# A two-layer decoder trunk with expert retrieval: choosing the experts of a token tile by groups of heads, and the second tile's one step later

## What is computed

```python
h = _rms(x, g_mix); z = h @ w_in            # q/k/v, latents, conv channels, gates
y_d = differential attention; y_m = latent attention; y_c = short gated convolution
x = x + (sum_i sigmoid(gate_i) * (branch_i @ W_branch_i)) @ w_out
x = x + _peer(_rms(x, g_ffn), w_query, sub_keys, u_experts, v_experts)
x = x + jax.nn.sigmoid(_rms(x, g_ple) @ w_ple_gate) * (p_i @ w_ple_proj)
```

```python
q = (hc @ w_query).reshape(T, PEER_HEADS, 2, PEER_DK)               # 8 heads, 2 halves
s = jnp.einsum('thpd,phnd->thpn', q, sub_keys)                      # 128 keys a half
top_s, top_i = lax.top_k(s, K_SUB)                                  # 16 of 128
cand = (top_s[:, :, 0, :, None] + top_s[:, :, 1, None, :])          # 16 x 16 sums
best_s, best_c = lax.top_k(cand.reshape(..., 256), PEER_TOPK)       # 16 of them
expert = i1 * N_KEYS + i2; gate = jax.nn.softmax(best_s, axis=-1)
act = jax.nn.gelu(jnp.einsum('thkd,td->thk', u_tab[expert], hc))
out = jnp.einsum('thk,thkd->td', gate * act, v_tab[expert])
```

## Time and profile before

| | |
|---|---|
| Median of 3 runs (lowest, highest) | 3680.86 us (3680.29, 3682.27) |
| Profiled execution: its time, its span | 3685.88 us, 3684.1 us |
| Busy: TensorE, VectorE, ScalarE, POOL | 2899.2, 2490.3, 1434.9, 1336.4 us |
| Moved by DMA | 1298.54 MB, mean 352 GB/s over the span |
| of it gathered rows | 1073.81 MB |
| Granted clock of TensorE, mean | 0.898 |

### The profile page before, as it was taken

How to read it: one execution, slowest core, us unless ns; L and a number is a source line. 1 busy time by engine, 2 the same in 40 slices (tenths; PEclk the granted TensorE clock), 3 DMA queues, 4 the chain that set the end, 5 groups by cost and what they waited for, 6 DMA issues and landing times. The chain is left out here.

```text
span 3684.1 us, 28841 instructions
## 1 busy us (share of the span) xinstructions
PE 2899.2 (79%) x8144; PEld 1478.3 (40%) x8144; DVE 2490.3 (68%) x5165; ACT 1434.9 (39%) x3967; POOL 1336.4 (36%) x1033
## 2 busy tenths in 40 slices
PE   7689948878988788867988788878998785656556
PEld 4454714535436333533436334535436331112112
DVE  1311386877667877777667877877667976777775
ACT  2230224457433344457433344457433342224222
POOL 0000033434333443345332443344332444555553
PEclk9879979989999999889999999989999897778777
DMA  4213379999998999999998999999998999999996
GB/s 155 83 69 139 113 310 376 390 363 387 401 381 343 387 398 403 387 390 405 420 376 346 391 408 398 370 384 421 417 389 342 399 399 421 422 421 397 422 421 254
DMA packets 182400, 1298.54 MB, mean 352 GB/s; under 512 B 20320, under 2 KB 21856, under 8 KB 26592
## 3 DMA queue, kind: packets, MB, share of 16 engines
q0 software_dynamic: 147456, 1073.81, 71.9%
q1 hardware_dynamic: 34784, 222.88, 15.3%
HBM read 1294.51 MB, written 2.10 MB: 352 GB/s over the span
## 5 line engine op out<-in xcount | busy, mean ns | idle before, releaser
L548 POOL DMA_INDIRECT ring<-in_uv,experts x1024 | 1333.9, 1303 | 2299.6 <-DVE x L1261 906.2
L1378 PE MATMUL ps_sum<-ring,diag 128*128 128x512 f32 x2120 | 1216.0, 716 | 622.7 <-ACT diag L815 621.9
L1252 DVE SCALAR_TENSOR_TENSOR ring<-ring,h_ffn 128x1024 f32<-128x1024 f32 x1024 | 1233.8, 1220 | 207.5 <-DMA ring<-in_uv,experts 201.3
L1378 PEld LDWEIGHTS ps_sum<-ring,diag 128*128 128x128 f32 x2120 | 437.7, 221 | 1288.2 <-ACT diag L815 892.9
L1261 DVE SCALAR_TENSOR_TENSOR x<-ring,weight,x 128x1024 f32<-128x1024 f32 x494 | 633.2, 1282 | 234.4 <-ACT weight L809 234.3
L807 ACT ACTIVATE dots<-dots 128x1 f32<-128x1 f32 x1024 | 205.3, 200 | 1346.7 <-DVE ring L1252 1344.4
L1516 PE MATMUL ps_act<-area_h,wt 128*128 128x256 f32 x1536 | 347.5, 385 | 2.4 <-ACT area_h L564 2.4
L1644 PE MATMUL ps_act<-wt,area_h 128*128 128x512 f32 x768 | 339.2, 596 | 9.2 <-DMA wt<-in_weights 9.1
L1516 PEld LDWEIGHTS ps_act<-area_h,wt 128*128 128x128 f32 x1536 | 295.0, 193 | 59.2 <-issue 15.6
L809 ACT ACTIVATE weight<-dots,gate 128x1 f32<-128x1 f32 x1024 | 301.6, 295 | 33.3
L1440 PE MATMUL ps_act<-wt,area_h 128*128 128x512 f32 (+1 forms) x704 | 303.7, 591 | 4.8 <-ACT area_h L564 4.5
(11 more groups left out here) (187 smaller groups left out, 2086.8 us busy)
## 6 DMA issues: line engine op xcount, KB each, us to landing
wt<-in_weights SPq DMA_DIRECT2D x190, 1024.0 KB
ring<-in_uv,experts POOLq DMA_INDIRECT x1024
wt<-in_weights SPq DMA_DIRECT2D x11, 512.0 KB
wt<-in_weights SPq DMA_DIRECT2D x4, 768.0 KB
x<-in_x SPq DMA_DIRECT2D x4, 512.0 KB, 5.0
area_y<-in_keys SPq DMA_DIRECT2D x4, 512.0 KB, 9.7
area_f<-in_keys SPq DMA_DIRECT2D x4, 512.0 KB, 10.7
area_f<-in_ffn_rows SPq DMA_DIRECT2D x4, 512.0 KB, 3.2
```

What stands on the lines that cost most here:

```text
L548: pool.indirect_dma_start(ring[:, row.slot, :], None, a[f"uv{row.step // 2}"][:, :], bass.IndirectOffsetOnAxis(ap=experts[:, row.step % 2, ...
L1252: dve.scalar_tensor_tensor(u, u, 1.0, h_ffn[:, row.tile, :], ALU.mult, ALU.mult, accum_out=dots[:, row.j:row.j + 1]).then_inc(dots_ready, 1)
L1378: ins = pe.matmul(ps_sum[:, b, :], diag[:, row.pe_before % DIAGS, :], ring[:, row.slot, D + b * 512:D + (b + 1) * 512], start=row.pe_first ...
```

## The change

The choice is cut otherwise. A part is now (`kind`, first head, end head): `first` makes the sums, maxima and indices of a group of heads, `second` the removal and second eight of it, and four `final` parts follow for all heads. Tile 0 of every chunk is chosen in the groups 0 to 3, 4 and 5, 6 and 7 (`early`), and the first four parts stand behind the ranks of heads 3, 4, 5 and 6. Tile 1 of chunks 1 and 2 is chosen in the step after, in eight parts that stand between `ple_out` and the second `conv_c`, without rows of their own (`topk_late`); that of chunk 3 at the beginning of step 3, with rows; that of chunk 0 where it was. Some temporaries of the choice move from `area_h` to `area_b` and `area_y`. `PE_PART` of `query`, `scores` and `rank` goes from 0.5 to 0.9, and the row costs of `query` and `rank` go up a little.

```diff
-TOPK_OPS = [3, 16, 16, 16, 4, 4, 4]
+LISTS = {"all": (0, 4, 8), "early": (0, 4, 6, 8)}
+FINAL_OPS = [9, 4, 4, 4]
+def parts_of(way):
+    ends = LISTS[way]
+    out = [(kind, lo, hi) for lo, hi in zip(ends, ends[1:]) for kind in ("first", "second")]
+    return out + [("final", i, 0) for i in range(len(FINAL_OPS))]
...
-    "out": 3.5, "ffn_norm": 4, "query": 1.6, "scores": 0.5, "rank": 1.6, "topk": 3,
+    "out": 3.5, "ffn_norm": 4, "query": 2, "scores": 0.5, "rank": 1.8, "topk": 3, "topk_late": 0,
...
-           "out": 0, "query": 0.5, "scores": 0.5, "rank": 0.5, "topk": 1, "taps": 1, "diff_sq": 1, "diff_norm": 1,
+           "out": 0, "query": 0.9, "scores": 0.9, "rank": 0.9, "topk": 1, "taps": 1, "diff_sq": 1, "diff_norm": 1,
...
+def behind(stages, places):
+    out = []
+    for st in stages:
+        out.append(st)
+        for place, more in places:
+            out += more if st == place else []
+    return out
...
+    if stage[0] == "topk":
+        kind, lo, hi = stage[3]
+        return 2 if kind == "final" else 0.6 * (hi - lo)
...
-        out += [("rows", done, i) for i in range(2)] + tail(done + 1, 0)
+        out += choice(step, 1) + [("rows", done, i) for i in range(2)] + tail(done + 1, 0)
...
-        out += choice(d, 0)
-        if d:
-            out += choice(d, 1)
+        first = choice(d, 0, way="early")
+        out = behind(out, [(("rank", d, i), [part]) for i, part in zip((3, 4, 5, 6), first)]) + first[4:]
+    if 0 < step < STEPS - 1:
+        late = choice(step, 1, "topk_late")
+        turn = [st for st in out if st[0] == "diff_turn"][-1]
+        places = [("ple_out", done, 0), ("x_norm", d), ("qkv", d, 0), ("qkv", d, 0), ("qkv", d, 2), turn, ("conv_c", d, 0), ("conv_c", d, 1)]
+        out = behind(out, [(place, [part]) for place, part in zip(places, late)])
...
-        top_f = area_h[:, 512:768].rearrange("p (h c k) -> p h c k", h=HEADS, c=2)
+        top_f = area_b[:, 4096:4352].rearrange("p (h c k) -> p h c k", h=HEADS, c=2)
...
-                        sp.wait_ge(dve_ops, WHERE[("topk", STEPS - 1, 1, len(TOPK_OPS) - 1)].dve + 4)
+                        sp.wait_ge(dve_ops, WHERE[("topk", STEPS - 1, 1, LAST_PART)].dve + 4)
```

More of the change, by code:

```diff
@@ L133, in tiles_done, with choice @@
     return [("for_act", at.evacs + 2)]
-def choice(d, t):
-    return [("topk", d, t, part) for part in range(len(TOPK_OPS))]
+def choice(d, t, name="topk", way="all"):
+    return [(name, d, t, part) for part in parts_of(way)]
+def behind(stages, places):
[5 more added lines that the diff above has]
+    return out
 def mix(d, pairs):
@@ L798, in _ @@
                          branch_more=nothing, mix_turn=mix_turn,
-                         out=out, rows=nothing, tail_norm=tail_norm, tail_out=tail_out, ffn_norm=ffn_norm, query=query, scores=scores, rank=nothing, topk=topk)
+                         out=out, rows=nothing, tail_norm=tail_norm, tail_out=tail_out, ffn_norm=ffn_norm, query=query, scores=scores, rank=nothing, topk=topk, topk_late=topk)
             rows = Rows()
@@ L1230, in _ @@
                          branch_first=branch, branch_more=branch,
-                         mix_turn=nothing, out=out, rows=nothing, tail_norm=tail_norm, tail_out=tail_out, ffn_norm=ffn_norm, query=nothing, scores=nothing, rank=rank, topk=topk)
+                         mix_turn=nothing, out=out, rows=nothing, tail_norm=tail_norm, tail_out=tail_out, ffn_norm=ffn_norm, query=nothing, scores=nothing, rank=rank, topk=topk, topk_late=topk)
             rows = Rows()
@@ L1713, in _ @@
                          branch_more=branch, mix_turn=mix_turn,
-                         out=out, rows=nothing, tail_norm=tail_norm, tail_out=tail_out, ffn_norm=ffn_norm, query=query, scores=scores, rank=nothing, topk=nothing)
+                         out=out, rows=nothing, tail_norm=tail_norm, tail_out=tail_out, ffn_norm=ffn_norm, query=query, scores=scores, rank=nothing, topk=nothing, topk_late=nothing)
             pe.wait_ge(consts_loaded, 16 * N_CONSTS)
```

78 lines of the change are left out of this document (42 added, 36 removed).

## The result

The changed kernel takes 3700.65 us (median of five, 3695.68 to 3707.47) against 3681.34 for the kernel before: ratio 1.0051, 95% interval 1.004 to 1.0062. It is slower by half a per cent. The profiled execution has a time of 3707.47 us and a span of 3705.5 against 3684.1; it is the slowest of the five, 6.8 us above their median, so a few us of what its windows show belong to this execution alone. Both kernels move 1298.5 MB.

What follows compares the result with a forecast made beforehand. The kernel was taken as a stream near its limit with holes where another engine paces it. Prologue -6, step 0 (18 + 2 - 30), steps 1 and 2 (22 + 2 - 30) each, step 3 +4: -24, so 3657 us; range 3608 to 3706.

Steps and rivals of the forecast that it cites:

- C: Queries, ranks and choices of steps 0 to 2, up to the next step's first row: 191 against 221.4 us, -30 each.
- A of steps 1 and 2: From a step's first row to the end of `mla_out`: twelve more rows, emptied ring, late choice; 441 us, +22 each.
- Two signs that I had named for being wrong: A growing by more than 34 us in steps 1 and 2, or C shrinking by less than 20.
- A of step 0: First row to the end of `mla_out`: 11 rows more, 28 us of hole left; 450 us, +18.
- B: Mixing, `out` and `ffn_norm`: three rows more, added by VectorE; +2 us (0 to 7.5).
- Prologue: Its end, with the choice's groups of heads between ranks: ids at 484.8 instead of 490.64 us, -6 (bounds -4, -9).
- Step 3: Restart 2.5 us, and its choice between 17 rows +1.5: +4 us.
- The restart at a step's start: First gather only behind the ids, ring empty: row 256 lands 5.1 us or 2.1 rows later; some 2.5 us VectorE wait.
- `diff_turn`: In A: TensorE starts about 2 us late behind the first final part; 3 us in all for choice work not covered.
- The slower rival: Late choice keeps the stream's hole open: A 454 (+35) to 475 (+56), time 3694 to 3736 us; chance 0.25.
- larger gain: Rival: A's hole closes to 3 us, C takes 180; -29 in each of three steps, -91 in all, 3590 us; chance 0.12.

Runs made afterwards that it cites:

- the opposite edit: The kernel before with nine tenths of the rows of the queries, scores and ranks added by TensorE in place of half: 3712.44 us (1.0092).
- the run of 3610: Changed kernel, groups of heads between ranks only in the prologue, half of the queries' rows on TensorE, late choice kept: 3609.76 us (0.9812).
- the two remedies: Changed kernel with no rows for the four parts between ranks (3645.91 us alone) and half of the queries' rows on TensorE (3671.07 alone); both: 3630.19 us.
- the choice at the step's start: Changed kernel with the second tile's choice of steps 1 and 2 at the step's very start, with rows of its own: 3725.75 us (1.012).

## Why the prediction was wrong

The direction was wrong. The time lies in the range, 44 us above the forecast, but that is the width of the range and luck: C fell short of its forecast by 30 us, A of steps 1 and 2 went 44 us beyond it, and the other terms came out 28 us better than forecast for reasons that the sum didn't hold. Either of the first two, had it been right, would have made the sum a gain. Two signs that I had named for being wrong came: A grew by more than 34 us in steps 1 and 2, and C shrank by less than 20 in step 0. Point by point:

- **C, -30 a step: failed, -17 to -22, and for a reason that the sum couldn't hold.** I added TensorE's work up to the last scores as if it ran on ("eight periods of 7.07 + 1.05 + 1.3 and 39 rows of 1.75 = 144 us") and took the parts between the ranks as VectorE work under its waits. With `ffn_norm` and rank 7 that made 154 us; the queries took 166, and the rest of C 34 where I had 37 (the 9.1 us from the ids to the next row were 7.6). The 1.3 us, a wait for the diagonal in every period, was an assumption (the one wait shown is 1.74): 10.4 us in all, measured 21.2. What was missing is order: nine tenths of the rows put up to three between a product and the scores that VectorE waits for, and the parts' rows must be added before the next product while their inner products stand behind a rank. Each engine then waits for the other (VectorE 55.5 us for scores, TensorE 21.2 us for diagonals, up to 4.5 at a time). The two edits that take rows out of these places give -55 and -30 alone and -70 together; the opposite edit costs the kernel before +32. With the groups behind the ranks and half of the rows on VectorE, C takes 173 to 176 us (the run of 3610), so the 191 was neither what the change does nor what its rows need.
- **A of steps 1 and 2, +22: failed, +37 and +51.** The least time was nearly right (430 where I had 426.2). The term that was wrong is the hole, taken as 12: it is 25.9 and 43.7 and was 27.8 and 28.0, so it did not shrink. I had let it because "each stage now takes more" rows; with the late choice left out it is still 19 and 29. The choice itself costs 6 us a step and not 3. TensorE's waits for diagonals in A of step 1 grew from 65 to 81 us, but 76.5 of it stay without the choice, so it isn't the choice that makes them; their cause is open, and with it why the hole stayed.
- **A of step 0, +18: failed the other way, +7.4.** Here the hole did shrink, from 37.8 to some 20 (439.8 us at 403 GB/s), where I had kept 28.
- **B, +2: -5.4 to -1.3.** The 10.9 us of hole took the three rows and all that was left.
- **Prologue -6: -3.8** in this pair of executions, whose last rank ended at 473.82 where I had 471.95, so the ids came at 486.95 and not at 484.8. One pair doesn't tell that from -6: the first inner product came at 488.9 to 497.2 us in the 17 profiled executions with this prologue (median 493.3), and at 497.1, 498.5 and 502.4 in the three with the one before. That is -5, inside its bounds. **Step 3 +4: +0.9**: the choice there runs with no hole.
- **The restart at a step's start** happened as described (ids behind the last row, first gather 0.55 us later, a product that waits 2.21 us), but filling the ring won nothing: its stream time vanishes in holes of stages behind it. The 2.1 rows that I charged for it did not show in the time.
- **`diff_turn`, 3 us**: it starts at 1452.27 without a wait; nothing is lost there.
- **The slower rival** named the right size (454 and 475 us for A, 3694 to 3736) with the wrong cause: "the late choice keeps the stream's hole open" is worth 13 to 17 us of the time. Without it the changed kernel would still not be faster than before (3688).
- A slip that nothing hangs on: under "larger gain" three steps of -29 and the rest make -89 us, not -91.

Why A of step 2 keeps 29 us of hole where step 0 has 20 isn't settled. Its attention is the same size. It has the stages `ple_norm` and `ple_out` besides, and step 0 has instead the choice of a tile with rows that TensorE adds (87 rows of A on TensorE against 75); no run varied that. Nor is it settled why the two remedies overlap by 14 us.

## What to carry to other kernels

Where two in-order engines hand work to each other, the sum of each one's work is no forecast: write out one period of both queues, item by item, and look for an item that stands behind the partner's long work on one queue and ahead of the partner's next input on the other. Splitting filler work between the engines by share moves such items; splitting it by place (none between a product and the result that the other engine waits for) won 10 and 14 us here at the same number of rows, and taking just the worst placed ones from TensorE won 41. And when a shared stream bounds a kernel, account for an edit in holes, stage by stage: rows taken out of a stage that keeps its length are paid for in full elsewhere.

## What the hardware showed

Nothing of the chip itself surprised. Every version has a stretch in which the stream reached 420 to 422 GB/s (B of step 1 in the changed kernel, 421; the 45.8 us of the choice at the step's start, 422), so the 2.485 us per MiB of the prediction held. The executions of the kernel after lay within 12 us of each other and those of the kernel before within 2 in the first session; in later sessions the kernel before spread over 12 to 22 us too, so the scatter is no mark of the change.
